# Four input projections of a hybrid layer as seven block products each, h scaled by its root first, silu by the sigmoid function

## The reference, cut to what matters

```python
h = rmsnorm(x, norm_mix_g)
proj = h @ w_in
u_h, gate_b, gate_c, q, k, v, g_out, gk_low = jnp.split(proj, splits, axis=-1)
u = gate_c * u_h
conv = conv_w[0]*u_pad[:, 0:s] + conv_w[1]*u_pad[:, 1:s+1] + conv_w[2]*u_pad[:, 2:s+2]
y_conv = gate_b * conv
...                                     # GLA: o from q, k, v and the decays of gk
y_gla = rmsnorm(o, gla_norm_g) * jax.nn.silu(g_out)
x = x + concatenate([y_conv, y_gla]) @ w_out
x = x + moe(rmsnorm(x, norm_ffn_g))     # top 4 of 32, gate and up, down
```

## Time and profile before

| what | us |
|---|---|
| median of three runs | 1035.74 |
| the profiled execution, its own time | 1037.62 |
| its span, first to last instruction | 1035.9 |
| PE busy, of the span | 1009.3 |
| DVE busy | 244.4 |
| ACT busy | 140.9 |
| bytes moved, 423.92 MB, mean rate | 409 GB/s |

### The profile page before, as it was taken

The page is one execution under the profiler, slowest core; times in us unless marked ns, Lnnn a source line. Parts: engine busy times, 40 slices in busy tenths (PEclk is TensorE's granted clock), DMA queues, the critical chain, the costliest instruction groups (busy, mean ns, idle before and its releaser), DMA issues.

```text
span 1035.9 us, 12057 instructions
## 1 busy us (share of the span) xinstructions
PE 1009.3 (97%) x4820; PEld 412.6 (40%) x4820; DVE 244.4 (24%) x622; ACT 140.9 (14%) x281; POOL 7.7 (1%) x27
## 2 busy tenths in 40 slices
PE   9999999999999999999999999999999999999997
PEld 7688843333333333333333333333333333333333
DVE  2264132222222221222211222211212121222122
ACT  1100121111111111111111111111111111111112
POOL 1000000000000000000000000000000000000000
PEclk9999999999999999999999999999999999999999
DMA  9953999999999999999999999999999999999995
GB/s 376 404 232 118 428 391 423 429 426 426 434 431 430 428 433 433 428 434 433 429 433 434 428 431 433 430 431 431 433 429 433 434 428 434 425 428 426 427 420 235
DMA packets 24712, 423.92 MB, mean 409 GB/s; under 512 B 3048, under 2 KB 3696, under 8 KB 6384
## 3 DMA queue, kind: packets, MB, share of 16 engines
q1 hardware_dynamic: 23328, 420.78, 95.6%
q10 hardware_dynamic: 1360, 2.79, 0.7%
HBM read 422.51 MB, written 1.05 MB: 409 GB/s over the span
## 4 chain that ended last, share of the span: by engine, by line
PE 75%; DMA 23%; issue 1%; DVE 0%; SPq 0%; ACT 0%; POOL 0%; ACTq 0%; PEldq 0%; DVEq 0%; POOLq 0%
PE bank L1529 31%; DMA ring<-in_w_expert 22%; PE bank L1549 18%; PE bank L1255 5%; PE bank L1415 4%; PE y L1593 4%; PE bank L1568 3%; PE y L1378 2%; PE bank L1471 1%; PE bank L1239 1%; PE bank L1378 1%; DMA g_h<-in_x_cols 1%; PE bank L1574 1%; PE bank L1651 1%; PE bank L1265 1%
## 5 line engine op out<-in xcount | busy, mean ns | idle before, releaser
L1529 PE MATMUL bank<-ring,x_t 128*64 128x512 f32 x1984 | 447.1, 597 | 0.0
L1549 PE MATMUL bank<-ring,act 128*64 128x512 f32 x992 | 230.8, 596 | 12.3 <-DMA ring<-in_w_expert 12.3
L1529 PEld LDWEIGHTS bank<-ring,x_t 128*64 128x64 f32 x1984 | 133.9, 136 | 261.9 <-issue 258.1
L1549 PEld LDWEIGHTS bank<-ring,act 128*64 128x64 f32 x992 | 68.3, 137 | 143.6 <-issue 141.2
L1092 DVE TENSOR_TENSOR gu_b<-bank,bias_t 128x512 f32<-128x512 f32 x64 | 44.2, 691 | 327.5 <-PE bank L1568 327.5
L718 ACT COPY gu_sb<-bank 128x512 f32<-128x512 f32 x64 | 37.5, 586 | 222.8 <-PE bank L1529 222.8
L1593 PE MATMUL y<-z,p_t 64*128 64x512 f32 x248 | 61.6, 615 | 0.0
L1415 PE MATMUL bank<-x_sb,p_row 128*64 128x512 f32 x256 | 60.6, 593 | 0.0
L1045 DVE TENSOR_TENSOR x_t<-bank,cols 128x512 f32<-128x512 f32 x30 | 20.8, 692 | 165.1 <-PE bank L1471 165.1
L1255 PE MATMUL bank<-g_h,ring 128*128 128x256 f32 x256 | 56.1, 380 | 0.0
L1031 DVE TENSOR_SCALAR p_row<-slot,rank,rstd 128x64 f32<-128x64 f32 x62 | 16.6, 312 | 164.5 <-PE bank L1574 164.5
(11 more groups left out here) (229 smaller groups left out, 404.9 us busy)
## 6 DMA issues: line engine op xcount, KB each, us to landing
ring<-in_w_expert SPq DMA_DIRECT2D x66, 4096.0 KB, 35.5
ring<-in_w_expert SPq DMA_DIRECT2D x48, 2048.0 KB, 18.9
ring<-in_w_expert SPq DMA_DIRECT2D x18, 1024.0 KB, 11.2
ring<-in_w_in SPq DMA_DIRECT2D x4, 2048.0 KB, 26.8
ring<-in_w_out SPq DMA_DIRECT2D x2, 2048.0 KB, 27.3
ring<-in_w_in SPq DMA_DIRECT2D x2, 1024.0 KB, 13.9
ring<-in_w_expert SPq DMA_DIRECT2D x4, 512.0 KB, 5.1
ring<-in_w_down_last SPq DMA_DIRECT2D x4, 512.0 KB, 28.6
```

What stands on the lines that cost most here:

```text
L1529: ins = mm(bank[h][a * SLOTS:(a + 1) * SLOTS, :], x_t_of(it)[:, k, :], w[:, kk, a, :], start=k == 0, stop=k == KT - 1)
L1549: ins = mm(bank[0][a * SLOTS:(a + 1) * SLOTS, :], act_of(it)[:, k, :], w[:, kk, a, :], start=k == 0, stop=k == KT - 1)
```

## The change

The 1024 by 512 weights of a chunk are seen as two halves of D (rows) by two halves of the columns, and h as two halves of D by two halves of the tokens (128 each). Each of GG, UU, CC and BB then takes seven products of blocks instead of eight; a block product is 8 `mm` of 128 by 128 weights with 128 tokens. For that, DVE makes four sums of weight blocks in each chunk (`sum_1` to `sum_4`, each 128 x 1024, one in `w_sum`, three in place in the ring's slot) and, once, four sums of h blocks (`h_sums`, 128 x 512 each). ACT copies four products of each chunk out of PSUM (`keep_part`), DVE adds them to the four quadrants of the result (`quad_11` to `quad_12`), for CC and BB with a further product each.

h is multiplied by `bc` once, in place (`scale_h`), after QK, the low-rank gate and VV have used it; the products by `bc` and `bc2` at the four projections and in the convolution are gone. silu is ACT's Sigmoid, between two table loads, and one DVE instruction.

The new tiles `h_sums`, `parts_of` and `w_sum` lie in slot 6 until the last quadrant, so chunk g = 5 waits for all sixteen quadrants, and so does g = 8. SP's order puts chunk g = 7 (slot 8, free after o) between g = 2 and g = 3.

```diff
-            for g, (it, j) in enumerate(LOAD_ORDER):
+            for g in [0, 1, 2, 7, 3, 4, 5, 6] + list(range(8, len(LOAD_ORDER))):
+                it, j = LOAD_ORDER[g]
...
-                        sp.wait_ge(s_pj, PROJ.index((g + 1, 1)) + 1)
+                        sp.wait_ge(s_prod, PRODUCTS * g)
                     elif g == 5:
-                        sp.wait_ge(s_dec, 3)
-                        sp.wait_ge(s_ex, 3)
-                        sp.wait_ge(s_kt, 1)
+                        sp.wait_ge(s_quad, QUADS * len(BLOCKED))
...
-            act_e.wait_ge(s_pkd, 5)
-            act_e.activation(sil[:, :, :], g_t[:, :, :], ACT.Exp, scale=-1.0).then_inc(s_sg, 1)
+            def keep_part(c, p, product, src):
+                act_e.wait_ge(s_prod, PRODUCTS * c + product)
+                act_e.copy(parts_of[:, p, :, :], src).then_inc(s_part, 1)
+
+            def keep_parts(c):
+                act_e.wait_ge(s_quad, QUADS * c)
+                keep_part(c, 0, 1, acc_a)
+                keep_part(c, 1, 3, acc_c)
+                keep_part(c, 2, 4, acc_d)
+                keep_part(c, 3, 5, acc_a)
+
+            keep_parts(0)
+            act_e.preload_act_table_set("sigmoid_and_others")
+            act_e.wait_ge(s_quad, QUADS)
+            act_e.activation(sil[:, :, :], g_t[:, :, :], ACT.Sigmoid).then_inc(s_sg, 1)
+            act_e.preload_act_table_set("natural_log_exp_and_others")
+            keep_parts(1)
...
+            def scale_h(t):
+                dve.wait_ge(s_pj, PROJ.index((VV, t)) + 1)
+                c = slice(t * P, (t + 1) * P)
+                dve.tensor_tensor(h_t[:, :, c], h_t[:, :, c], bc[:, c]..., ALU.mult).then_inc(s_hs, 1)
+
+            def sum_2(c):
+                dve.wait_ge(s_sum, SUMS * c + 1)
+                dve.wait_ge(s_prod, PRODUCTS * c + 1)
+                dve.tensor_tensor(w_block(c, 0, 0), w_sum[:, :, :], w_block(c, 0, 0), ALU.subtract).then_inc(s_sum, 1)
...
-            link(dve.tensor_scalar(sil[:, :, :], sil[:, :, :], 1.0, None, ALU.add))
-            link(dve.reciprocal(sil[:, :, :], sil[:, :, :]))
-            link(dve.tensor_tensor(sil[:, :, :], sil[:, :, :], g_t[:, :, :], ALU.mult))
-            link(dve.tensor_scalar(sil[:, :, :], sil[:, :, :], cols[:, COL_GLA:COL_GLA + 1], None, ALU.mult))
+            dve.scalar_tensor_tensor(out=sil[:, :, :], in0=sil[:, :, :], scalar=cols[:, COL_GLA:COL_GLA + 1], in1=g_t[:, :, :],
+                                     op0=ALU.mult, op1=ALU.mult).then_inc(s_sil, 1)
...
+            def multiply(acc, w, h, first, last):
+                for m in range(2):
+                    for k in range(4):
+                        ins = mm(acc[:, m, :], w[:, k, m * P:(m + 1) * P], h[:, k, :],
+                                 start=first and m == 0 and k == 0, stop=last and k == 3, skip_group_check=True)
+                ins.then_inc(s_prod, 1)
+
+            def project_blocked(c):
+                quads, parts, sums = QUADS * c, PARTS * c, SUMS * c
+                ...
+                multiply(acc_a, w_block(c, 0, 0), h_block(0, 0), True, False)
+                multiply(acc_b, w_block(c, 0, 1), h_block(1, 0), True, True)
+                pe.wait_ge(s_sum, sums + 1)
+                ...
+                multiply(acc_c, w_sum, h_sums[:, 0, :, :], True, False)
+                ...
+                multiply(acc_d, w_block(c, 1, 0), h_sums[:, 1, :, :], True, False)
+                pe.wait_ge(s_sum, sums + 3)
+                pe.wait_ge(s_part, parts + 1)
+                ...
+                multiply(acc_a, w_block(c, 0, 0), h_sums[:, 2, :, :], False, True)
+                pe.wait_ge(s_part, parts + 3)
+                ...
+                multiply(acc_d, w_block(c, 1, 1), h_sums[:, 3, :, :], False, True)
+                pe.wait_ge(s_sum, sums + 4)
+                ...
+                multiply(acc_c, w_block(c, 0, 1), h_block(1, 1), False, True)
```

More of the change, by code:

```diff
@@ new lines, in sum_4, with quadrant @@
+            def sum_4(c):
+                dve.wait_ge(s_sum, SUMS * c + 3)
+                dve.wait_ge(s_prod, PRODUCTS * c + 2)
+                dve.tensor_tensor(w_block(c, 0, 1), w_block(c, 0, 1), w_block(c, 0, 0), ALU.subtract).then_inc(s_sum, 1)
+            def quadrant(c, m, t, product, src, part):
+                dst = quad_of((g_t, u_t, u_pad[:, :, TAPS - 1:], y_t)[c], m, t)
+                dve.wait_ge(s_prod, PRODUCTS * c + product)
+                ins = dve.tensor_tensor(dst, src, parts_of[:, part, :, :], ALU.add)
+                if BLOCKED[c] in (CC, BB):
+                    link(ins)
+                    ins = dve.tensor_tensor(dst, dst, quad_of(u_t if BLOCKED[c] == CC else conv, m, t), ALU.mult)
+                ins.then_inc(s_quad, 1)
@@ L924, in _, with convolve @@
             keep_scores(1)
-            keep_scaled(6)
+            sum_2(1)
+            sum_4(1)
+            quad_11(1)
+            sum_1(2)
             dve.wait_ge(s_sg, 1)
-            link(dve.tensor_scalar(sil[:, :, :], sil[:, :, :], 1.0, None, ALU.add))
-            link(dve.reciprocal(sil[:, :, :], sil[:, :, :]))
-            link(dve.tensor_tensor(sil[:, :, :], sil[:, :, :], g_t[:, :, :], ALU.mult))
-            link(dve.tensor_scalar(sil[:, :, :], sil[:, :, :], cols[:, COL_GLA:COL_GLA + 1], None, ALU.mult))
[L935 to L941, removed]
+            dve.wait_ge(s_quad, QUADS)
+            dve.scalar_tensor_tensor(out=sil[:, :, :], in0=sil[:, :, :], scalar=cols[:, COL_GLA:COL_GLA + 1], in1=g_t[:, :, :],
+                                     op0=ALU.mult, op1=ALU.mult).then_inc(s_sil, 1)
+            sum_3(2)
+            quad_22(1)
+            quad_21(1)
+            quad_12(1)
+            def convolve(i):
                 for j in range(TAPS):
@@ L951, in _ @@
                     link(ins)
-                link(dve.tensor_tensor(conv[:, r, :], conv[:, r, :], twice(bc), ALU.mult))
+            sum_2(2)
+            sum_4(2)
+            dve.wait_ge(s_quad, 2 * QUADS)
+            quad_11(2)
+            sum_1(3)
+            sum_3(3)
+            quad_22(2)
+            quad_21(2)
+            dve.wait_ge(s_quad, 2 * QUADS + 3)
+            convolve(1)
+            quad_12(2)
+            dve.wait_ge(s_quad, 2 * QUADS + 4)
+            convolve(0)
+            sum_2(3)
+            sum_4(3)
+            dve.wait_ge(s_sil, 1)
             for i in range(2):
@@ L960, in _ @@
                                   ALU.mult).then_inc(s_ygla, 1)
[L961 to L964, removed]
+            quad_11(3)
+            quad_22(3)
+            quad_21(3)
+            quad_12(3)
             dve.wait_ge(s_late, 16 * 2)
@@ L1280, in _ @@
             ins.then_inc(s_bc, 1)
[L1282 removed]
+            project_v(0, range(2))
             pe.wait_ge(s_pkd, 1)
```

188 lines of the change are left out of this document (120 added, 68 removed).

## The result

| | before | after |
|---|---|---|
| median of five runs of each, on the same chip, us | 1036.40 (1035.66 to 1037.91) | 1030.73 (1030.61 to 1032.56) |
| span of the profiled execution, us | 1035.9 | 1028.9 |
| ratio, 95% interval | | 0.9948 (0.9936 to 0.9959) |

The kernel became faster by 5.67 us. Two more comparisons, which follow, each against the kernel before on its own chip, gave 5.19 and 5.24. The forecast was 1029.7, within 1027.6 to 1033.4.

What follows compares the result with a forecast made beforehand. The expert-weight stream, starting with item 0 on PE, was taken to set the end. Block products gain 5.2 us, the queue 0.8, stalls and waits cost 0: 1035.74 - 6.0 = 1029.7 us, range 1027.6 to 1033.4.

Steps and rivals of the forecast that it cites:

- What bounds the kernel: The expert-weight stream sets the end; PE waits 12.3 us for it; the stream's unbroken start depends on item 0's start.
- The block products, 5.2: In GG, UU, CC and BB, 112 records at 0.1117 us take 12.51 us a chunk, not 13.81; four save 5.2 us.
- More than forecast: Rival: block products run at half the present pace, 0.1079 us, as if loads did not count; 7.7 us gained, chance 0.06.
- the bound of 0.115: Lower bound for the block products: at L1393's pace of 0.115 us a record, four chunks gain only 3.7 us.
- No stalls, sum 0: In the four chunks PE never waits for DVE's sums and quadrants or ACT's copies; cost 0.
- the slack of 1.6 at the third product: In GG the first sum of h is ready at 38.8 us, 1.6 us before PE's third block product needs it.
- The waits: Some twenty further PE semaphore waits, already satisfied, cost 0; at most 0.05 us each, 1 us.
- gain lost: Rival: slow in-place sums in the mixer, or waits and a late queue restart, lose part of the gain; chance 0.10.
- Seams that drain: Rival: each of 28 block-product seams costs PE 0.36 us, 10 us in all, ending at 1039.7; chance 0.08.
- The queue term, 0.8: Four chunks, not five, go out after BB, so g = 12's first quarter lands 3.5, not 4.3, after issue: 0.8 us gained.
- The end moves by as much as this landing moves: Claim that the kernel's end shifts one for one with the landing of g = 12's first quarter, 144.4 us before the change.
- From there on there is no gap: Claim that after g = 12's first quarter lands, at 144.4 us before the change, the weight stream runs unbroken.

Runs made afterwards that it cites:

- Two more comparisons: The changed kernel run again, unaltered, against the kernel before on each chip: 1031.37 against 1036.56 us, and 1031.0 against 1036.24 us.
- the 64 columns: Changed kernel with each block-product matmul moving 64 columns instead of 128, half the result left out: 12.45 against 12.51 us a chunk, 1030.97 us.
- two pairs of runs: Changed kernel with SP's old load order, 1031.63 us against 1031.37 unaltered; kernel before with only the new load order, 1036.44 against 1036.56.

## Why the prediction was right, and where it was not

**What bounds the kernel: right.** Over fourteen traces T0 - v ranges over 13.9 us, by the length of the chunks, while the end comes 895.2 to 897.2 us after T0. The end moves one for one with item 0's start, within 1 us. PE's 12.3 us of waits for it are still there, 11.3.

**The block products, 5.2: right.** T0 - v fell by 5.23. The pace of 0.1117 from L1340 holds for 448 records. "More than forecast", at 0.108, is out, by 112 records in 12.51 us and by the 64 columns. So is the bound of 0.115.

The Trainium skill's 107 ns for such a load ("TensorE: Matmul & The Clock Gate", section "LDWEIGHTS (loading the stationary operand)") would make GG 11.95 us, an estimate. The measured 12.51, 112 ns a load, decides.

**No stalls, sum 0: right.** No wait on DVE or ACT beyond 0.2 up to BB's end; the slack of 1.6 at the third product was measured as 1.7 twice. The waits, taken at 0 with 1 us as bound, are 0. Of the rival "gain lost", the half in the mixer did not occur: all four sums ran at 1.22 us in GG, not at 1.6 or more. The loss of 2.2 us that the rival gives for 1.8 has no working: four sums 0.575 us longer overdraw a slack of 1.6 by 0.7.

**Seams that drain: refuted.** The price of 0.36 us at each of 28 seams would have put T0 10 us later; 112 records follow one another without a gap, and 112 further waits change T0 by 0.01.

**The queue term, 0.8: in all likelihood mis-sized.** The step behind it is "The end moves by as much as this landing moves". The landing of g = 12's first quarter did move, from 5.45 to 4.60 us after T0. But the quarter stands in a stretch in which the stream is short of released slots before it (284 GB/s) and slow behind it (379 and 399 GB/s), so "From there on there is no gap" does not hold: the kernel before too moves only 338 GB/s in those 10 us. The 0.85 us there can no longer be told from nothing at the load of T0 + 19.4, and the medians put it at 0.1 to 0.3 at the end by two pairs of runs, inside their noise. I had taken one landing for the beginning of the unbroken stream. It belongs at 0 to 0.3, so the sum is 5.2 to 5.5. Three comparisons gave 5.67, 5.19 and 5.24, in the mean 5.4; T0 accounts for 5.2 of each by their traces. That the first lies nearest to the forecast 6.0 is chance: its own interval is 4.2 to 6.6 us.

**The forecast of 1029.7** lay 1.0 below the 1030.73 measured. Of that, 0.66 is the kernel before, 1036.40 on this chip against the 1035.74 from which the sum set out; 0.33 is the sum itself, 6.0 against 5.67.

## What to carry to other kernels

Count a blocked product in weight loads, not in arithmetic: with 128 moving columns in fp32 each record costs its load, 0.112 us, and the scheme gains only because seven block products, 112 short records (12.51 us), still beat 64 long ones (13.81); eight would lose. Where a stream of transfers sets the end, look for the first load after which it never starves again, and let only what moves that one count; a transfer sent early into an idle stretch bought nothing measurable here, where the next ones wait for slots that PE frees. And an instruction that costs nothing now, such as a 6.56 us reciprocal on an engine that no one waits for, has a price once that engine feeds the bound one.

## What the hardware showed that was not expected

POOL's two mask instructions, together, grew from 1.22 us in the kernel before to 3.25, and one DVE sum beside them from 1.22 to 1.54. POOL before, then POOL and DVE in the changed kernel:

```profile
56.73 1.22 POOL L585 TENSOR_SCALAR_AFFINE_SELECT sc<-sc 128x512 f32<-128x512 f32 x2 [38.60 <-DVE sc L905]
```

```profile
54.90 3.25 POOL L607 TENSOR_SCALAR_AFFINE_SELECT sc<-sc 128x512 f32<-128x512 f32 x2 [38.54 <-DVE sc L1019]
```

```profile
56.12 1.54 DVE L930 TENSOR_TENSOR ring<-ring 128x1024 f32<-128x1024 f32 x1
```

The sums with two operands in SBUF begin as the scores are out, just when POOL masks them. The mask is done at 58.15 and needed at 63.7, so it cost nothing here. The kernel with the second product made twice separates the two, since its second sum of UU comes later:

```profile
56.02 2.27 POOL L607 TENSOR_SCALAR_AFFINE_SELECT sc<-sc 128x512 f32<-128x512 f32 x2 [39.08 <-DVE sc L1019]
```

```profile
57.98 1.38 DVE L930 TENSOR_TENSOR ring<-ring 128x1024 f32<-128x1024 f32 x1 [0.78 <-PE bank L1363]
```

There the first mask instruction, beside the sum that starts at 55.98, takes 1.68 us as in the changed kernel; the second, which starts at 57.66 with DVE idle, takes 0.63 instead of 1.61, as in the kernel before. So the DVE sums are what lengthens the masks. The Trainium skill, "SBUF — State Buffer", section "🔬 SBUF: two separate sides", says that a VectorE operation with two SBUF inputs and a GpSimd operation that reads SBUF lock each other out of a shared port; by that rule, the trace agrees: in the changed kernel the two masks end at 56.58 and 58.15, each 0.5 us after the sum beside it, at 56.08 and 57.65.

Also new: a weight load of 128 by 128 in fp32 keeps its pace of 0.111 to 0.112 us under matmuls of 128 and of 64 columns alike, and a wait on PE that is already met has no measurable price.
